# One transformer layer pair on one core: value products a step later, query tiles turned inside the chunked attention, a mask added by TensorE

## The reference, cut to what matters

```python
# first block: six modulation vectors, an input product, two attentions
mod = jnp.dot(jax.nn.silu(c), w_ada[l]) + b_ada[l]
h = modulate(rmsnorm(x, g_attn_norm[l]), sh_a, sc_a)
proj = jnp.dot(h, w_in[l])                     # q_lat 256, kv_lat 128, k_rope 32, ca_qkv 1536
q = jnp.dot(rmsnorm(q_lat, ...), w_q_up[l])    # 8 heads of 96, normed, the last 32 by rope
kv = jnp.dot(rmsnorm(kv_lat, ...), w_kv_up[l]) # keys 64 (+ 32 of k_rope), values 64
o_mla = mla_attention(q, k, v)                 # latent attention, block-causal, softmax
o_ca = chunk_attention(cq, ck, cv, rel_bias)   # chunked attention: + bias, mask, softmax, 8 heads of 64
# second block: stick-breaking attention of 8 heads, for each query
z = q @ k.T * scale
mask = kpos[None, :] < qpos[:, None]
lneg = jnp.where(mask, jax.nn.log_sigmoid(-z), 0.0)
tail = lax.cumsum(lneg, axis=3, reverse=True) - lneg
w = jnp.where(mask, jnp.exp(jax.nn.log_sigmoid(z) + tail), 0.0)
```

## Time and profile before

| | |
|---|---|
| median of 3 runs | 2313.58 us (2311.64 to 2328.39) |
| profiled execution | 2316.41 us, span 2314.6 us |
| TensorE busy | 2231.7 us (96%) |
| VectorE busy | 1825.5 us (79%) |
| ScalarE busy | 1451.9 us (63%) |
| mean granted clock of TensorE | 0.983 of full |

### The profile page before, as it was taken

One profiled execution on the slowest core, in us unless ns is written; L12 is line 12 of the kernel. 1 busy time (PEld: TensorE's weight loads), 2 busy tenths in 40 slices (PEclk: granted clock), 3 DMA queues, 4 the chain that ended last, 5 costly groups with the idle time before them and its releaser, 6 DMA issues.

```text
span 2314.6 us, 31537 instructions
## 1 busy us (share of the span) xinstructions
PE 2231.7 (96%) x10491; PEld 1802.2 (78%) x10491; DVE 1825.5 (79%) x1869; ACT 1451.9 (63%) x1697; POOL 395.3 (17%) x310
## 2 busy tenths in 40 slices
PE   6998899999999999998999999999999999999998
PEld 3875677888888887676788888888888888888866
DVE  6887545555723494857999999999999999999964
ACT  3355534333513344534888888888888888888863
POOL 1000000000000000001344233233333323323310
PEclk9999799999999999999999999999999999999999
DMA  9440303322122230145999999999999999999960
GB/s 345 155 159 1 128 11 99 109 90 93 64 100 73 89 109 28 46 158 192 391 389 384 395 389 383 397 383 391 394 387 378 397 385 387 392 390 387 369 229 37
DMA packets 185162, 560.42 MB, mean 242 GB/s; under 512 B 12991, under 2 KB 37474, under 8 KB 185093
## 3 DMA queue, kind: packets, MB, share of 16 engines
q1 hardware_dynamic: 172325, 523.64, 59.1%
q0 software_dynamic: 12768, 35.86, 6.0%
HBM read 543.18 MB, written 26.23 MB: 246 GB/s over the span
## 4 chain that ended last, share of the span: by engine, by line
PE 86%; DVE 8%; ACT 3%; issue 2%; DMA 1%; SPq 1%; ACTq 0%; DVEq 0%
PE bank L2039 12%; PE bank L2041 12%; PE bank L2045 12%; PE bank L1622 6%; PE bank L1624 6%; PE bank L1623 6%; PE bank L1601 4%; PE bank L2034 4%; PE bank L2032 4%; PE bank L2033 4%; PE bank L1844 3%; PE bank L1845 3%; PE bank L1846 3%; PE bank L1706 2%; PE bank L1686 1%
## 5 line engine op out<-in xcount | busy, mean ns | idle before, releaser
L2803 DVE TENSOR_TENSOR w_lo<-stage,w_hi 128x2048 fp32r<-128x2048 f32 x396 | 903.6, 2348 | 17.9 <-ACT w_hi L1399 17.7
L1399 ACT ACTIVATE w_hi<-stage 128x2048 fp32r<-128x2048 f32 x396 | 732.4, 1910 | 6.6 <-DMA stage<-in_w_up_gate 6.6
L2039 PE MATMUL bank<-w_hi,xeT_hi 128*128 128x512 f32 x792 | 247.4, 394 | 5.5 <-ACT bank L1406 3.8
L2041 PE MATMUL bank<-w_hi,xeT_lo 128*128 128x512 f32 x792 | 244.4, 390 | 0.0
L2045 PE MATMUL bank<-w_lo,xeT_hi 128*128 128x512 f32 x792 | 212.6, 390 | 0.0
L995 POOL PARTITION_BROADCAST bias_all<-bias_raw x134 | 206.8, 1609 | 5.4 <-DMA bias_raw<-in_b_up_gate 3.1
L1624 PE MATMUL bank<-half_top,hT_low 128*128 128x512 f32 (+1 forms) x480 | 185.7, 387 | 0.0
L2045 PEld LDWEIGHTS bank<-w_lo,xeT_hi 128*128 128x128 f32 x792 | 149.3, 188 | 31.1
L2041 PEld LDWEIGHTS bank<-w_hi,xeT_lo 128*128 128x128 f32 x792 | 149.0, 188 | 31.2
L2039 PEld LDWEIGHTS bank<-w_hi,xeT_hi 128*128 128x128 f32 x792 | 146.1, 188 | 34.2 <-issue 4.0
L1622 PE MATMUL bank<-half_top,hT_top 128*128 128x512 f32 (+1 forms) x416 | 161.2, 387 | 2.6 <-DVE ring_low L2231 1.4
(11 more groups left out here) (495 smaller groups left out, 4482.2 us busy)
## 6 DMA issues: line engine op xcount, KB each, us to landing
stage<-in_w_up_gate SPq DMA_DIRECT2D x264, 1024.0 KB, 12.0
stage<-in_w_down SPq DMA_DIRECT2D x132, 1024.0 KB, 13.0
ring<-in_w_ada SPq DMA_DIRECT2D x12, 2048.0 KB, 9.5
ring<-in_w_up SPq DMA_DIRECT2D x22, 1024.0 KB, 7.6
ring<-in_w_in SPq DMA_DIRECT2D x10, 2048.0 KB, 7.9
ring<-in_w_out SPq DMA_DIRECT2D x4, 2048.0 KB, 11.2
ring<-in_w_down SPq DMA_DIRECT2D x4, 2048.0 KB, 8.1
stage<-in_w_ple_gate SPq DMA_DIRECT2D x4, 1024.0 KB, 13.7
```

What stands on the lines that cost most here:

```text
L1399: fn(w_hi[top_of(h)][:, :], src[:, :], ACT.Copy).then_inc(s_hi, 1)
L2039: mm(bank[b][:, :], hi[:, k0 + k, :], wh[:, k, at_[b]:at_[b] + CW], start=first and k == 0, stop=False, skip_group_check=banks[0] < 4)
L2041: mm(bank[b][:, :], lo[:, k0 + k, :], wh[:, k, at_[b]:at_[b] + CW], start=False, stop=False, skip_group_check=banks[0] < 4)
L2803: tt(w_lo[h][:, :], stage[h][:, :], w_hi[top_of(h)][:, :].bitcast(FP), ALU.subtract).then_inc(s_lo, 1)
```

## The change

Three edits, and some fillers less.

1. Fillers: "ada" (18) and both inside the first norm (5 and 14) are gone, "win" has 4 for 8.
2. PV_LAG is 4 for 3 in kinds 0 and 1, and OT_LAG moves with it.
3. The queries' transposes of heads 4 to 7 stand at steps 18, 20, 26 and 28 of the chunked attention, those of heads 0 to 3 at steps 33 to 36 (TURNED: step, head, bank). ScalarE copies each a step later. Behind the attention only the keys are turned, and their copies are split: even heads VectorE, odd heads ScalarE.
4. In the stick-breaking attention each scores product is followed by one of 128 columns in bf16, identity times mask, added into the bank. `ident_top` and `mask_top` are the upper halves of the f32 words of `ident` and `negm`, read with a stride of two. VectorE's addition and its semaphore are gone, and ScalarE waits for the scores themselves.

```diff
--- before.py
+++ after.py
@@ -201,6 +201,7 @@
     conb = at(96 * KB, [P, packs["b"][1]], name="conb")
     def cb(n):
         return conb[:, where[n][0]:where[n][0] + where[n][1]]
+    ident_top, mask_top = (a.bitcast(BF).rearrange("p (a b) -> p a b", b=2)[:, :, 1] for a in (ident, cb("negm")))
     sbq = at(R, [P, NT, CW], name="sbq")
     sbk = at(R + 8 * KB, [P, NT, CW], name="sbk")
     sbqT = at(R + 16 * KB, [P, NT, S], name="sbqT")
@@ -430,11 +431,12 @@
         order.append((("warm", name), rot[0] % 8 if b is None else b))
 
 
-    WARM = {"ada": 18, ("norm", 0, 1): 5, ("norm", 0, 2): 14, "win": 8, "mT": 12, ("step", 1, 2): 4, "o1": 3, "wout": 6,
+    WARM = {"win": 4, "mT": 12, ("step", 1, 2): 4, "o1": 3, "wout": 6,
             ("norm", 1, 0): 10, ("norm", 1, 3): 7, "up": 14, ("step", 2, 3): 11, ("step", 2, 4): 8,
             "o3": 7, "wout2": 7, "rank": 18, "rows": 18}
+    TURNED = {18: (4, 7), 20: (5, 7), 26: (6, 7), 28: (7, 7), 33: (0, 0), 34: (1, 1), 35: (2, 2), 36: (3, 0)}
     LAG = {0: 2, 1: 2, 2: 3}
-    PV_LAG = {0: 3, 1: 3, 2: 5}
+    PV_LAG = {0: 4, 1: 4, 2: 5}
     OT_LAG = {k: n + 3 for k, n in PV_LAG.items()}
 
     def attention_order(kind):
@@ -455,6 +457,8 @@
                 product(("oT", kind, (s - OT_LAG[kind]) // H - 1), 7)
             if kind == 0 and s in SUMMED:
                 product(SUMMED[s], 6 + s % 2)
+            if kind == 0 and s in TURNED:
+                product(("mT", 0, TURNED[s][0]), TURNED[s][1])
 
     def norm_order(nz):
         for t in range(NT):
@@ -468,7 +472,6 @@
     product(("vecs",))
     product(("adaT", 0))
     product(("adaT", 1))
-    kept_warm("ada")
     product(("ada", 3))
     product(("adaT", 2))
     product(("adaT", 3))
@@ -493,9 +496,8 @@
     ADAT = (6, 7, 8, 9)
     product(("adaT", 6))
     attention_order(0)
-    for qk in range(2):
-        for h in range(H):
-            product(("mT", qk, h))
+    for h in range(H):
+        product(("mT", 1, h))
     kept_warm("mT", next(b for label, b in order if label == ("mT", 1, 0)))
     attention_order(1)
     kept_warm("wout")
@@ -616,7 +618,6 @@
     s_mod, s_sq, s_xn = sem("modulation"), sem("x_rms"), sem("x_normed")
     s_ms, s_rt, s_nrm = sem("head_mean_square"), sem("head_rms"), sem("head_normed")
     s_max, s_P, s_pv = sem("row_max"), sem("probs"), sem("pv_done")
-    s_msk = sem("stick_masked")
     s_o = sem("attention_out")
     s_conv, s_cg, s_act, s_xr = sem("conv_done"), sem("gate_silu"), sem("mlp_act"), sem("x_updated")
     s_rqd, s_kd, s_rsq = sem("rqd"), sem("k_decayed"), sem("ret_squares")
@@ -1133,8 +1134,7 @@
                     if kind == 2 and s < 4 * H:
                         n = (s // H + 1) * P
                         W1 = sbl[s % 4]
-                        act_e.wait_ge(s_msk, s + 1)
-                        b = bank[bank_of[("S", 2, s)][0]]
+                        b = full(act_e, ("S", 2, s))
                         if s >= 4:
                             act_e.wait_ge(s_P, 4 * H + s - 3)
                             full(act_e, ("T", 2, s - 4))
@@ -1236,11 +1236,17 @@
                 if s == 26:
                     roots(3)
                     roots(4)
+                if s - 1 in TURNED:
+                    q_turned(TURNED[s - 1][0])
+
+            def q_turned(h):
+
+                copy_out(mT[0][:, h, :], ("mT", 0, h), lambda b: b[0:QK, :], vec[0:QK, VMQ:VMQ + 1])
 
             mod_columns(6)
             attention(0, PR1, PT1, while_chunked)
-            for h in range(H):
-                copy_out(mT[0][:, h, :], ("mT", 0, h), lambda b: b[0:QK, :], vec[0:QK, VMQ:VMQ + 1])
+            for h in range(1, H, 2):
+                copy_out(mT[1][:, h, :], ("mT", 1, h), lambda b: b[0:QK, :], vec[0:QK, VMK:VMK + 1])
             def while_attending(s):
 
                 if 8 <= s < 12:
@@ -1683,7 +1689,10 @@
                         t, h = divmod(s, H)
                         n = (t + 1) * P
                         b = acquire(("S", kind, s))
-                        publish(mm(b[:, 0:n], q_of(h, t), k_of(h, n), start=True, stop=True), ("S", kind, s))
+                        ins = mm(b[:, 0:n], q_of(h, t), k_of(h, n), start=True, stop=kind < 2)
+                        if kind == 2:
+                            ins = mm(b[:, t * P:n], ident_top, mask_top, start=False, stop=True)
+                        publish(ins, ("S", kind, s))
                     i = s - LAG[kind]
                     if ("step", kind, s) in WARM:
                         keep_warm(("step", kind, s))
@@ -1742,7 +1751,6 @@
 
             ada_T(0, modrow)
             part_T(1)
-            keep_warm("ada")
             slot = arrived(("ada", 3))
             wv = part(slot, 0, KT, CW)
             b = acquire(("ada", 3))
@@ -1796,17 +1804,23 @@
                 if s in SUMMED:
                     name, c = SUMMED[s]
                     part_T(c) if name == "adaT" else part_rows(c)
+                if s in TURNED:
+                    pe.wait_ge(s_nrm, 4)
+                    latent_T(0, mq, TURNED[s][0])
+
+            def latent_T(qk, src, h):
+
+                b = acquire(("mT", qk, h))
+                for t in range(NT):
+                    ins = tr(b[0:QK, t * P:(t + 1) * P], src[:, t, h, :])
+                publish(ins, ("mT", qk, h))
 
             pe.wait_ge(s_kz, 2)
             attention(0, lambda h, t: caqT[:, h // 2, t * P:(t + 1) * P], lambda h, n: cakz[:, h, 0:n],
                       lambda h, j: cav[:, j, h * HD:(h + 1) * HD], PR1, PT1, oc, while_chunked)
-            for qk, src in enumerate((mq, kv[:, :, :, HD:])):
-                pe.wait_ge(s_nrm, 4 + qk)
-                for h in range(H):
-                    b = acquire(("mT", qk, h))
-                    for t in range(NT):
-                        ins = tr(b[0:QK, t * P:(t + 1) * P], src[:, t, h, :])
-                    publish(ins, ("mT", qk, h))
+            pe.wait_ge(s_nrm, 5)
+            for h in range(H):
+                latent_T(1, kv[:, :, :, HD:], h)
             keep_warm("mT")
             for qk in range(2):
                 for h in range(H):
@@ -1894,6 +1908,7 @@
                 for t in range(NT):
                     taken(pe, ("sbT", qk, t))
             pe.wait_ge(s_kz, 4)
+            pe.wait_ge(s_conb, 16)
             attention(2, lambda h, t: sbqT[:, h // 2, t * P:(t + 1) * P], lambda h, n: sbkz[:, h, 0:n],
                       lambda h, j: sbv[:, j, h * HD:(h + 1) * HD], PR2, PT2, o2)
 
@@ -2306,9 +2321,6 @@
                             link(ve.memset(b[0:HD, n - HD:n], NEG))
                             link(ve.tensor_reduce(c, b[:, 0:n], AX, ALU.max, negate=True))
                             ts(c, c, hs[:, 3 * 32 + s:3 * 32 + s + 1], None, ALU.mult).then_inc(s_max, 1)
-                        else:
-                            b = full(dve, ("S", 2, s))
-                            tt(b[:, t * P:n], b[:, t * P:n], cb("negm"), ALU.add).then_inc(s_msk, 1)
                     if kind == 2 and 0 <= s - 1 < 4 * H:
                         stick(s - 1)
                     i = s - PV_LAG[kind]
@@ -2524,7 +2536,7 @@
                         ins.then_inc(s_nrm, 1)
 
             attention(0, PR1, PT1, oc, while_chunked)
-            for h in range(H):
+            for h in range(0, H, 2):
                 label = ("mT", 1, h)
                 b = full(dve, label)
                 take(ts(mT[1][:, h, :], b[0:QK, :], vec[0:QK, VMK:VMK + 1], None, ALU.mult), label)
```

## The result

The changed kernel took **2292.77 us** (median of 4, 2287.86 to 2297.18), the kernel before in the same comparison 2315.68 (2311.64 to 2328.39): ratio 0.9898, interval [0.9862, 0.9933]. The profiled execution took 2287.86 us with a span of 2286.0. Against the profiled one of before that is 28.6 us less. The same kernel, run again later, gave 2292.97 us and 0.9894 [0.9876, 0.9912], with a profiled execution of 2292.72 us.

A forecast was written before the change was run, and what follows sets the result against it. TensorE's chain of waits (86% of the span) was taken as the bound. Terms 1.3 - 5.0 - 6.0 - 2.6 - 2.6 = -14.9 us gave 2301.5 or 2298.7, stated 2300; own range 2293 to 2307 (56%), wider 2287 to 2312 (8 in 10).

The forecast's parts named there:

- rival B: Latent attention: TensorE keeps the 2.4 GHz clock, 8 us less than 2300, so 2292 us; chance 18%.
- Front: Up to the first input product: work begins 1.3 us earlier, a low clock costs 2.6; +1.3 us (-1.3 to +2.2).
- Lag, chunked: Chunked attention: value products a step later lose part of 11.0 us of waits for copies; -5.0 us (0 to -11.0).
- turning: Chunked attention: latent query transposes moved into it, 3.5 us behind it go, two heads cost 0.9; -2.6 us.
- Lag, latent: Latent attention: value products a step later, 5 us from the 7.4 us wait, 1 from earlier scores; -6.0 us.
- Rival A: Chunked and latent attention: the waits only move, to the transposes; without both lag terms 2311 us; chance 16%.
- signs of a wrong forecast: Among them: TensorE's idle time in the chunked and latent attentions stays at 12.7 and 8.2 us under another name.
- The other signs: Value products' wait below 3 us, first product near 52.4 us, chunked stretch about 77, latent 71; untouched stretches only shift.
- Rival C: First input products: low clock lasts through the first two chunks (40 us), slower at 2319 us; chance 5%.
- Rival D: Turning buys nothing or the mask product costs 0.23 us: 2303 to 2305 us; chance 5%.
- Mask: Stick-breaking attention: VectorE drops 32 additions of 0.20 us, TensorE gains products of 0.10 us each; -2.6 us.

The follow-up runs named there:

- front-only kernel: The kernel before with only the filler edit (18, 5 and 14 taken out, 'win' 4 for 8): 2315.79 us, 0.9999.
- lag-only kernel: The kernel before with only the value products a step later in chunked and latent attention (PV_LAG 4 for 3): 2295.22 us, 0.9909.
- spaced kernel: The changed kernel with the four early query turnings at steps 17, 21, 24, 28 instead of 18, 20, 26, 28: 2289.58 us, 0.9888.
- turning-only kernel: The kernel before with only the latent queries turned inside the chunked attention and the key copies split: 2314.37 us, 0.9991.
- without fillers: The changed kernel without its 12 fillers behind the turned keys and 4 in latent step 2: 2292.14 us, 0.9898.

## Why the prediction was right in its wider range and 7 us too high

The measured 2292.77 us lie within 2287 to 2312, but 0.2 us below the forecast's own 2293 to 2307, where rival B had put them (2292). So the number is owed to the room given to B and, in part, to luck: the sum said -14.9 us, the two profiles say -28.6 and the repeat -23.7, the medians -22.9. The front came out with the other sign, the other four terms with the forecast one; the latent term had the lag about right and left the clock out.

**Front (+1.3 predicted).** The mechanism held in five of seven profiles: an earlier first product, at a low clock. Both sizes were off. The product came 2.1 to 2.6 us earlier, not 1.3: the 1.51 us of ScalarE's idle time went, and its first block began 0.98 us sooner (40.36 to 39.38), because the transposes ahead of it, at the low clock before, ran at the high clock now. The low clock then costs 1.8 us, not 2.6. So the term is -0.2 to -0.8 where the start is cold and -2.5 or -2.6 where it isn't. The 18 fillers had their price as foreseen: without them the eight products of the fourth modulation chunk took 5.80 us for 3.67, the next product came at 35.23 for 34.30, and the cover hid it. The median of the front edit alone (0.9999) tells neither from zero.

**Lag, chunked (-5.0), and turning (-2.6).** Together -5.4 to -6.0 for -7.6, the second with as much low clock (10.2 us) as before. By groups: steps 0 to 23, forecast -4.2 (where eight steps at 0.3 were added as 2.2), took 46.3 before and 43.6 and 43.1 after; the front-only kernel, with the 6.8 us of low clock of the repeat, took 44.8, so the lag gave 1.7 to 2.6. Steps 24 to 30, forecast +0.1 (0.8 gained by the lag, 0.9 paid for two heads), took 19.7 before, 15.8 with the lag only, 19.3 and 19.2 after. (The lag-only kernel's 15.6 in its first eight steps had 10.2 us of low clock.) The lag was worth 3.9 there, at the high clock in both: the prediction had taken 0.1 us a step, though its own row showed 0.43 of wait in one, and 0.55 came. The change gave 3.5 of it back. TensorE stood 2.40 us for ScalarE to empty bank 7, a wait that the prediction did not list; some 0.9 were low clock; and the two heads themselves, charged 0.9, cost 0.2 by the spaced kernel (16.0 against 15.8). The rest of the stretch, forecast -3.5, fell by 2.3, and by 2.4 in the turning-only kernel: the four heads in the drain, charged nothing, cost 1.2 of their 1.8. That VectorE is the limit in the middle steps was right; between 189 and 200 us it was busy all but 0.7 us before and all but 0.6 after (VectorE alone, after):

```profile
189.00:200.00 11.00, 10.42 (x24) 1.00 0.01 2
```

**Lag, latent (-6.0): the term that failed, by what it left out.** Measured -16.2, in the repeat -11.9. The lag's own share is 5.5 to 7.9 us by the two estimates above, so its size, taken from the wait that would vanish (5 of 7.4 us, plus 1), was about right. What failed is that the sum left the clock of this stretch as it was: it was low for 34.1 us before and for 3.4 after (13.7 in the repeat), and that holds the rest, 8 to 11 us in the first profile and 4 to 6 in the repeat. Every group of steps got shorter, 9.0 to 6.2, 16.8 to 10.7, 20.7 to 18.2. What the lag would be worth with the clock high throughout in both stays open: no run of the old lag held it without fillers on the path.

One of the signs of a wrong forecast came true here, and misled: TensorE's idle time in the latent stretch stayed (8.2 us before, 7.4 after) under another name. The cause of that is the clock too. In the two kernels with 27.3 us of low clock each it fell from 8.3 (front only) to 5.1 (without fillers). With less of it TensorE's own work takes less time, and more of the wait for the other engines shows; that last step is argued, not shown. The other signs: the value products' wait is gone, as forecast; the first product stands at 51.1 for 52.4, the chunked stretch is 79.4 for 77, the latent 60.9 for 71; what lies between the stretches moved by under a microsecond.

**Rival B** (the latent attention keeps 2.4 GHz, -8, 18%) came true, at 8 to 11 us in the first profile and 4 to 6 in the repeat. The prediction took lag and clock for two things; on the chip the second came with the first, in all eight profiles with the lag and the fillers ahead and in none of the four with the old lag and the same fillers, so B was no rival of the forecast but its other half. What spoke against B, that the gapless stretch did not get the clock back by itself, is still so; the changed kernel never fell into it. **Rival A** (the waits only move, 16%) had the place right and the price wrong: 3.9 and 6.0 us of wait at the transposes, and the gain was there all the same. **Rival C** had its start (a low clock to 55.3 us) and not its length. **Rival D** fell, at 0.06 us a product.

**Mask (-2.6).** Measured -4.0, with that edit alone as well, and -5.3 in the five profiles without low clock in that stretch. By groups: 11.8 to 9.4, 11.9 unchanged, 15.4 to 14.0, 16.5 to 15.2. Steps 0 to 15, forecast -3.2, gave 2.5; VectorE, busy for 11.3 of 11.9 us in steps 8 to 15 in both kernels, stayed the limit there. Steps 16 to 30, forecast +0.6 (0.4 gained, 1.0 charged for TensorE), gave 2.6 instead: this is the part that was wrong. A product costs 0.06 us and not 0.10, and VectorE's addition stood between scores and sigmoid there too: ScalarE waited for it in 30 of 32 steps. To the end that the prediction used (the first turned output), 66.1 us became 60.8; it said 63.5.

By the Trainium skill ("TensorE: Matmul & The Clock Gate", Part 2, back-to-back gap) an isolated product of 128 columns would have been 56 ns; the measured 0.06 us agrees. The same section's figure for a stream in which each product has its weight load is 81 ns; here each has one too (0.10 us, mostly under the scores ahead of it), and the measured 0.06 us is below it. The same page's advice in "Why this matters for your kernels", to keep TensorE busy between bursts, holds only in part here. Taking the front fillers out cost nothing that the median can tell. The fillers ahead of the latent attention carry it through its narrow first steps (without them TensorE was busy for 20.80 of 21.00 us at 0.51), yet the kernel without them took 2292.14 us, as long as the one with them: against the repeat its chunked stretch is 1.6 us shorter, without the 12 fillers, and its latent one 1.8 us longer.

**Sum.** Front -2.6, chunked with turning -5.4, latent -16.2, stick-breaking -4.0 make -28.2 of the 28.6 us between the two profiles; the forecast was -14.9. Of the 13.3 us between, 10.2 are the latent term, 3.9 the front, 1.4 the mask, and -2.2 the chunked stretch with the turning. The repeat's profile, nearer the median, is 23.7 us below that of before: front -2.4 and then +1.8, chunked -6.0, latent -11.9, stick-breaking -5.3, and 0.1 in the rest.
